# A hybrid decoder step on one core: routing rebuilt, new tokens second in w_o, last logits from unnormed rows

## The reference

```python
    return m @ w_o, conv_new, s_new.astype(h.dtype), vn
...
    x = x + g1 * mix
    h = rmsnorm(x, norm2) * (1 + sc2) + sh2
    x = x + g2 * hier_moe(h, w_rg, b_rg, w_re, b_re, w_e_gate, w_e_up, w_e_down)
```

## Time and profile before

| | us |
|---|---|
| median of 3 runs | 1181.98 |
| lowest, highest | 1181.97, 1183.64 |
| the profiled execution | 1181.74 |
| its span, first to last instruction | 1180.0 |

### The profile page before, as it was taken

One profiled execution on the slowest core, in us unless ns is written; L12 is line 12 of the kernel. 1 busy time (PEld: TensorE's weight loads), 2 busy tenths in 40 slices (PEclk: granted clock), 3 DMA queues, 4 the chain that ended last, 5 costly groups with the idle time before them and its releaser, 6 DMA issues. The chain is left out here.

```text
span 1180.0 us, 15016 instructions
## 1 busy us (share of the span) xinstructions
PE 1069.7 (91%) x5862; PEld 703.7 (60%) x5862; DVE 560.2 (47%) x1109; ACT 250.2 (21%) x673; POOL 154.4 (13%) x299
## 2 busy tenths in 40 slices
PE   5999998999999999899999999999946998978786
PEld 3455777777777887887577777754423333322222
DVE  3123737467788494475754455443264111110126
ACT  3100010567622222464111010101110110100011
POOL 3000500012314000041100000100011211111101
PEclk8999998999999999899999999999967999998998
DMA  9995543252414443124462422359176999999975
GB/s 334 340 258 181 192 77 75 43 128 69 74 50 72 107 80 73 37 73 144 125 223 83 111 75 89 123 138 327 77 286 222 416 420 415 418 419 418 412 290 175
DMA packets 96852, 226.32 MB, mean 192 GB/s; under 512 B 21422, under 2 KB 40167, under 8 KB 84082
## 3 DMA queue, kind: packets, MB, share of 16 engines
q1 hardware_dynamic: 86998, 202.70, 52.5%
q10 hardware_dynamic: 4660, 12.75, 3.1%
q0 software_dynamic: 5120, 9.88, 2.3%
HBM read 210.60 MB, written 23.08 MB: 198 GB/s over the span
## 5 line engine op out<-in xcount | busy, mean ns | idle before, releaser
L2514 PE MATMUL ps<-w_gate_up,xT 128*64 128x512 f32 x528 | 129.5, 630 | 20.5 <-DMA w_gate_up<-w_e_up 20.5
L2514 PEld LDWEIGHTS ps<-w_gate_up,xT 128*64 128x64 f32 x528 | 41.2, 145 | 105.9 <-issue 76.8
L2676 DVE TENSOR_TENSOR act<-silu_gate,ps 128x256 f32<-128x256 f32 x17 | 7.1, 420 | 199.1 <-ACT silu_gate L2469 199.1
L695 PE MATMUL ps<-hT,w_ring 128*128 128x288 f32 x384 | 97.5, 414 | 3.7 <-PEq L105 3.7
L695 PEld LDWEIGHTS ps<-hT,w_ring 128*128 128x128 f32 x384 | 73.9, 195 | 23.9 <-issue 4.0
L2531 PE MATMUL ps<-w_down,actT 128*64 128x512 f32 x264 | 62.1, 599 | 8.8 <-DVE actT L2680 8.8
L1345 PE MATMUL ps<-hT,w_ring 128*128 128x288 f32 x264 | 67.8, 407 | 0.0
L1630 DVE SCALAR_TENSOR_TENSOR conv_y<-z_staged,convT,conv_y 128x600 f32<-128x600 f32 x72 | 59.7, 842 | 9.3 <-ACT conv_y L1080 7.5
L1345 PEld LDWEIGHTS ps<-hT,w_ring 128*128 128x128 f32 x264 | 49.4, 190 | 13.1 <-issue 0.5
L2531 PEld LDWEIGHTS ps<-w_down,actT 128*64 128x64 f32 x264 | 18.0, 136 | 41.2 <-issue 29.1
L2429 POOL DMA_INDIRECT pair_scratch<-y_block,pairs x16 | 16.0, 1003 | 200.7 <-ACT y_block L2477 200.7
(11 more groups left out here) (539 smaller groups left out, 1995.2 us busy)
## 6 DMA issues: line engine op xcount, KB each, us to landing
w_down<-w_e_down SPq DMA_DIRECT2D x32, 1024.0 KB, 23.6
w_ring<-w_in SPq DMA_DIRECT2D x15, 2048.0 KB, 13.8
w_gate_up<-w_e_gate SPq DMA_DIRECT2D x30, 1024.0 KB
w_gate_up<-w_e_up SPq DMA_DIRECT2D x30, 1024.0 KB
w_ada_slots<-w_ada SPq DMA_DIRECT2D x8, 2048.0 KB, 8.4
w_ada_slots<-w_ada SPq DMA_DIRECT2D x4, 1024.0 KB, 15.0
w_ring<-w_pa SPq DMA_DIRECT2D x2, 2048.0 KB, 7.9
w_ring<-w_pb SPq DMA_DIRECT2D x2, 2048.0 KB, 7.9
```

The source lines that it names most:

```text
L695: last = nc.tensor.matmul(psum[:, bank + hf, 0:HALF], w[:, c, 128 * q:128 * q + 128], x[:, c, HALF * hf:HALF * hf + HALF], start=c == 0, s ...
L2514: last = te.matmul(psum[side(u), s % 2, :], xT[:, s % 2, c, side(u)], gu[s % GU_BUFS][:, u, :, c, :], start=c == 0, stop=c == KC - 1)
```

## The change

In this order of the program:

- Positions: `ORDER = (0, 4, 1, 2, 3)`. Everything between w_o and the weights is kept by position, with the new tokens at position 1 and tile 3 last. `mod_new` is needed at position 1.
- TensorE's order in w_o: the transposes of position p-1 stand between the two halves of position p, its logits between the first and the last four chunks of the second half.
- Position 1 carries a 65th row, the prompt's shift, whose logits (with the bias) are spread to all rows by one matmul (`constant_logits`).
- The last tile's `h` is first written as x times scale, half by half (`scaled`), transposed and multiplied by the router from that; the row factor and the constant logits are applied on the 36 logits (L2551). The square is taken by halves, and GpSimd adds two instructions to join them.
- Routing by parts: `choose_experts` for three positions between the last tiles' residual adds, with its counts in memory of their own; `split_pairs` and `slot_rows_of` for these stand between the two halves of the last residual add. The same for the last two positions afterwards. Slots come from counts to which 1024 is added at every odd expert, so that one comparison finds side and slot, and the table of 16 columns holds the experts' first 64 rows only.
- Further blocks have a table of their own: `over_blocks` ahead of `weights`, `over_counts` and `over_pairs` behind the first `xT`, `over_slots` in block 1 ahead of its activation, 20 matmuls (`over_tables`) behind block 1's gate and up, two conversions behind them. GpSimd waits for it before the gather of block 8.
- SP: the first expert of `w_down` 3 is loaded without a wait; the second waits for `route_constants_used`, which VectorE gives at the end of `over_slots`. Block 3's `w_gate_up` stands behind it.
- GpSimd: `x_gathered` isn't cleared any more, `y_last` is cleared behind the first two gathers.

```diff
+ORDER = (0, 4, 1, 2, 3)
+EARLY_POS = 3
+SIDE = 1024.0
...
+        sp.wait_ge(xwd, 2)
+        sp.wait_ge(xsq, NT + 1)
         sp.wait_ge(x2st, 16 * NT)
         load_down(sp, m, ins, 2, (4, 5))
-        sp.wait_ge(h2tr, NT)
+        sp.wait_ge(h2d, NT)
+        sp.wait_ge(h2tr, END)
+        sp.wait_ge(x4tr, 2)
...
+        whole = range(KC)
+        o_half(0, 0, whole)
+        o_half(0, 1, whole)
+        o_new(1)
+        h2_transposes(0)
+        o_half(2, 0, range(0, 2))
+        logits(0)
+        o_half(2, 0, range(2, KC))
+        for p in range(2, NT):
+            if p > 2:
+                o_half(p, 0, whole)
+            h2_transposes(p - 1)
+            if p == 3:
+                constant_logits()
+            o_half(p, 1, range(0, 4))
+            logits(p - 1)
+            o_half(p, 1, range(4, KC))
+        early_counts()
+        last_transposes(0)
+        logits(END, range(0, 4))
+        table(0, EARLY_POS)
+        last_transposes(1)
+        logits(END, range(4, KC))
+        late_counts()
+        table(EARLY_POS, NT)
...
+        residual(0, 0)
+        residual(0, 1)
+        second_norm(0)
+        dve.wait_ge(nld, 32 * NB)
+        v.scalar_tensor_tensor(modn[0:64, 2, :], modn[0:64, 2, :], 1.0, n2[0:64, :], ALU.add, ALU.mult).then_inc(sc2, 1)
...
+        residual(3, 1)
+        dve.wait_ge(ld, 3)
+        choose_experts(nc, dve, m, r, 0, EARLY_POS, 0)
+        second_norm(3)
+        choose_experts(nc, dve, m, r, 0, EARLY_POS, 1)
+        residual(END, 0)
+        scaled(0)
+        split_pairs(nc, dve, m, r, 0, EARLY_POS)
+        add_logits(3)
+        slot_rows_of(nc, dve, m, r, 0, EARLY_POS, psum[:, 2, 0:96])
+        residual(END, 1)
+        scaled(1)
...
     def sync(sp):
-        sp.wait_ge(overd, 1)
-        load_down(sp, m, ins, 3, (6, 7))
+        load_down_of(sp, m, ins, 3, 0, 6)
+        sp.wait_ge(constd, 1)
+        load_down_of(sp, m, ins, 3, 1, 7)
...
+            last.then_inc(over_hot, 1)
+            dve.wait_ge(over_hot, 1)
+            v.nop().then_inc(constd, 1)
...
         def run(lo, hi):
+            if lo == 0:
+                over_blocks()
+                weights()
             x_evacuate(lo)
+            if lo == 0:
+                over_counts()
+                over_pairs()
             for s in range(lo, hi):
+                if s == 1:
+                    over_slots()
                 dve.wait_ge(sgd, s + 1)
+                if s == 1:
+                    over_table_columns()
```

More of the change, by code:

```diff
@@ new lines, in slot_rows_of, with step @@
+def slot_rows_of(nc, dve, m, r, lo, hi, counts):
+    v = nc.vector
+    at, n = slice(lo, hi), hi - lo
+    def step(i):
+        r.n += 1
+        i.then_inc(r.step, 1)
+        dve.wait_ge(r.step, r.n)
+    dve.wait_ge(r.counted, 1 if lo == 0 else 2)
+    for k in range(2):
+        i = v.tensor_tensor(r.prod[:, k, at, :], r.one[:, k, at, :], counts.rearrange("p (t e) -> p t e", e=NE), ALU.mult)
+        if k:
+            step(i)
+    for k in range(2):
+        i = v.tensor_reduce(r.v[:, k, at], r.prod[:, k, at, :], AX.X, ALU.add)
+        if k:
+            step(i)
+    for k in range(2):
+        for p in range(lo, hi):
+            last = v.tensor_scalar(r.onehot_slot[:, k, p, :], m.slots[:, :], r.v[:, k, p:p + 1], None, ALU.is_equal)
+    last.then_inc(r.hot, 1)
@@ L2096, in scalar, with square @@
-        square(0)
[L2097 to L2100, removed]
+        act.wait_ge(init, 3)
+        act.wait_ge(mld, 32)
+        act.wait_ge(win, 7 * PAIRS)
+        a.copy(h2[64:65, 1, :], modp[64:65, 1, :]).then_inc(shd, 1)
+        def square(p):
+            rows = PROWS[p]
+            act.wait_ge(x2d, 2 * p + 2)
+            if p:
+                act.wait_ge(xsq, p)
+            a.activation(junk[0:rows, :], m.x2[0:rows, ORDER[p], :], ACT.Square, accum_out=ss[0:rows, p:p + 1]).then_inc(xsq, 1)
@@ new lines, in keep_half @@
+        def keep_half(j):
+            act.wait_ge(x4tr, j + 1)
+            act.wait_ge(lmm, END)
+            a.copy(h2T[:, 4 * j:4 * j + 4, :].rearrange("p c t -> p (c t)"), psum[:, 4 + j, :]).then_inc(h2ev, 1)
+        square(0)
+        for p in range(1, END):
+            store_h2(p - 1)
+            keep_h2T(p - 1)
+            square(p)
+        store_h2(END - 1)
+        keep_h2T(END - 1)
+        square_half(0)
+        keep_half(0)
+        square_half(1)
+        keep_half(1)
+        store_h2(END)
@@ L2175, in tensor, with o_half @@
[L2175 to L2181, removed]
+        def o_half(p, j, cs):
+            tile, i = ORDER[p], 2 * p + j
+            if i >= 4 and cs[0] == 0:
+                pe.wait_ge(oev, i - 3)
+            for c in cs:
+                last = te.matmul(psum[:, i % 4, :], mT[:, c, tile_cols(tile)], wo[j][:, c, :], start=c == 0, stop=c == KC - 1)
+            if cs[-1] == KC - 1:
+                last.then_inc(omm, 1)
@@ new lines, in late_counts, with table @@
+        def late_counts():
+            pe.wait_ge(r.chosen, 2)
+            te.matmul(psum[:, 3, 0:32], r.strict, both[:, 3, :], start=False, stop=False)
+            te.matmul(cut(psum[:, 3, 32:96]), r.onesb, two(both[:, 3, :]), start=False, stop=False)
+            te.matmul(psum[:, 3, 32:64], r.strict, both[:, 4, :], start=False, stop=False)
+            te.matmul(psum[:, 3, 64:96], r.onesb, both[:, 4, :], start=False, stop=True).then_inc(r.counted, 1)
+        def table(lo, hi):
+            pe.wait_ge(r.hot, 1 if lo == 0 else 2)
+            for p in range(lo, hi):
+                rows = PROWS[p]
+                for k in range(2):
+                    for x in range(2):
+                        last = te.matmul(psum[:, 2, 128:144], r.onehot_slot[0:rows, k, p, :], r.parts[0:rows, x, k, p, :],
+                                         start=p == k == x == 0, stop=p == END and k == x == 1)
+            if hi == NT:
+                last.then_inc(r.tabled, 1)
@@ L2260, in vector @@
         dve.wait_ge(init, 2)
[L2262 to L2290, removed]
```

535 lines of the change are left out of this document (333 added, 202 removed).

## The result

| | before | after |
|---|---|---|
| median of all runs, us | 1181.82 (20 runs) | 1186.82 (20 runs) |
| lowest, highest | 1178.11, 1186.24 | 1182.84, 1190.53 |
| span of the profiled execution | 1180.0 | 1184.9 |

The ratio of after to before is 1.0043, with a 95% interval of 1.0032 to 1.0053: the changed kernel is slower by 5.0 us. The forecast was 1185.7, so the sign and the range hold, and the size was 1.3 us short if the two shifts are compared (+5.0 against +3.7).

What follows compares the result with a forecast made beforehand. The prediction took the restart of the expert weight stream and the bytes then left as the bound. Wait +2.5, 1 MB +2.5 and early traffic -1.3 gave 1181.98 + 3.7 = 1185.7 us, range 1179.0 to 1189.5.

Steps and rivals of the forecast that it cites:

- Link 1: TensorE's w_o stage, up to its last matmul: ends at 864.9 us instead of 861.4, +3.5 us.
- The stall on `mod_new`: In w_o, new tokens' modulation usable only at 810.5 us: VectorE stands 4.8 us, TensorE waits +3.4 us.
- Link 2: From the end of w_o to the routing table: 16.7 us instead of 29.8, `toks` ready at 881.6 us.
- Link 3: First gather, issued amid weight loads: 8.4 us to landing instead of 4.6, at 890.3 us instead of 896.05.
- The even share of bytes: First gather sharing engines evenly with the weights: 5.8 us, forecast 2.6 us lower; the prediction set it aside.
- Link 4: From the gather to the end of block 0's gate/up matmuls: unchanged 12.5 us, ending 902.8 us instead of 908.5.
- Link 5: SP waits for the signal after `over_slots`, at 911.1 us against a restart at 908.56; sum +3.7 us at the last weight.
- The 2.5 us for the 1 MB: Weight stream: 1 MB formerly loaded in idle time now goes in front of block 3, +2.5 us.
- The -1.3 us: Scatter 0 and gather 3 start some of their traffic before the weight stream restarts, -1.3 us.
- No stall: Rival in w_o: the modulation loads land before 806 us, -5.3 us, giving 1180.4 us; chance 15%.
- Light gather: Rival at the first gather: it takes only 4.6 to 7 us, giving 1181.9 to 1184.3 us; chance 15%.
- TensorE carries: Rival in the expert stage: the stream has slack and TensorE sets the end, giving 1178.3 us; chance 8%.

Runs made afterwards that it cites:

- the run with clear engines: Changed kernel, but SP waits for the first gather's landing before loading w_gate_up 2 and the first expert of w_down 3; 1182.39 us, ratio 0.9993.
- the early signal: Changed kernel with over_slots moved ahead of block 0's activation instead of in block 1; 1178.97 us, ratio 0.9975 to the kernel before.
- the second experiment: Changed kernel with SP's first expert weights held until the 16 loads of mod_new have landed; 1183.04 us, ratio 1.0004 to the kernel before.
- the late restart: Kernel before, with block 3's gate/up load also waiting for block 0's down matmuls; ratio 1.0047.

## Why the prediction was right, and where it was off

**Link 1, the end of w_o, +3.5: right, +3.6 by the traces** (865.02 - 783.94 = 81.1 us against 77.5). The stall on `mod_new` was foreseen in its place, and a little small: usable at 812.0 us instead of 810.5, so VectorE stood 6.2 instead of 4.8 us and TensorE 4.5 instead of 3.4. The last bytes moved later: the last packet of the sixteen loads ended at 811.4 us, where it had ended at 809.8 us in the kernel before (queue q10 had 1.04 MB by 809 us there, and 1.02 in the changed kernel), and VectorE started 0.6 us behind it, so the 1.5 us that were put behind 809 us fitted the kernel before. In three other executions of kernels with the same w_o it ended from 810.5 to 811.5 us. The slow clock came out as assumed, one stretch (four chunks in 5.40 us) in the place of the one before. That the total is right is in part luck: the 1.1 us more of waiting was made up by the set of transposes and logits that came into w_o, priced at 2.9 us. It is that of the new tokens, and took 0.92 + 0.92 us (820.82 to 821.74 and 826.98 to 827.90). The 0.5 us for constant logits and a wait for `h` was too much as well; the constant logits took 0.3 us and TensorE didn't wait there.

**Link 2, 16.7 us: right.** 865.02 to 881.68 us is 16.7. Small VectorE instructions at their interpolated pitch (64 elements 0.26 us, as 877.27, 877.53, 877.79 in the trace) carry such a sum well.

**Link 3, the gather, 8.4 us: mis-sized, 9.3 measured** (881.97 to 891.27 us). This is the first of the steps that made the forecast short. The mechanism was right and shown by the run with clear engines. The scatters of the earlier trace rows were the nearest rows but transfers in the other direction in a steadier stream; four kernels with weights in the queues now give 9.2 to 9.6 us from the request to TensorE's start. The even share of bytes that would have given 5.8 us was rightly set aside.

**Link 4, 12.5 us, "unchanged": 13.1.** It wasn't unchanged. TensorE had stood 10.0 us, the clock was at 0.50 up to 895 us, and the rows for the last block took 4.36 us. In the kernel before, behind a wait of 6.2 us, they took less, at a clock of 0.50 in the stretch from 895 to 900 us too:

```profile
897.86 3.64 PE L2540 MATMUL ps<-ident,slot_rows 128*128 128x128 f32 x20
```

The longer wait alone doesn't explain it. These twenty matmuls took 4.36, 4.14 and 4.23 us behind waits of 10.0 to 10.3 us, but with the early signal 3.44 us behind a wait of 9.9 us, and 3.37 to 3.69 us in the five kernels with waits of 5.0 to 6.4 us. What decides it stays open; the link was taken over from the kernel before without a range for its clock. The gate/up matmuls ended at 904.35 us, where 902.8 was forecast.

**Link 5, SP's new wait: right in mechanism, signal 1.5 us later for the reasons above.** From the end of gate/up to `over_slots` 3.1 us (3.0 forecast), `over_slots` 5.1 us (5.3), and 0.4 us more for issuing the 1 MB load ahead of block 3's, which the sum had left out. Restart 913.0 instead of 911.1 us. The 2.5 us for the 1 MB fits this kernel (208.1 - 205.6); the others with it gave 2.1 to 4.2. The -1.3 us, traffic of scatter 0 and gather 3 done before the restart, was too much. Scatter 0 was issued at 911.43 us, and nothing of it moved before 913.0 us; the first packet of the weights moved at 913.75. From 913 to 913.5 us GpSimd's queue moved

```profile
q0 software_dynamic: 46, 0.19, 95.3%
```

so some 0.7 us of the engines' time was used before the weights, not 1.3.

Sum by the traces: +4.4 (restart, from w_o's start) + 2.5 (1 MB) = +6.9, where +5.1 was measured; forecast +2.5 + 2.5 - 1.3 = +3.7. In the two profiles the difference lies behind the last request for weights: from there to the end the profile before took 65.9 us and the profile after 63.8. Over the nine profiles this stretch took 63.8 to 65.9 us without following the edits, and what sets it stays open. So the chain that the prediction follows was 3.2 us short (1.9 at the restart, 1.3 in the credit for early traffic), and 1.8 of them were given back by something that it doesn't hold.

**The rivals.** "No stall" was priced at -5.3 us; made true by the second experiment it gave -4.6, and -6.9 on top of the early signal. "Light gather" was priced at -3.8 us for a gather of 4.6 us; made true by clear engines (4.4 us) it gave -5.9 (3.7 to 8.1), and -4.4 on top of the early signal. "TensorE carries" is refuted by the late restart. The two prices were fair within the noise, for things that didn't happen by themselves. No run took the rebuilt routing itself back out; that it made the table 9.5 us earlier is read from the two traces.

## What to carry to other kernels

Where a prefetched stream stops for want of buffers, find what its restart waits for and read every wait that a change adds on the queue of that stream: a signal given 8 us later than needed cost more than the rebuilt routing had gained (9.6 us at the table, 4.9 behind the slower gather), and giving it from idle time of the same engine turned the change around. A small transfer on the critical path should be issued before, or into a gap between, the large ones; here both losses to load order (the modulation in w_o, the first gather) went away by holding back bulk loads that had slack. Price a shortened link together with its next link, since the gather now fell among weights that it had missed before.

## What the runs showed of the hardware

The modulation's 16 small loads slow down far more than their own bytes. In the changed kernel they run beside the weights, and with the modulation first they run alone. The stretches 786 to 799 and 800 to 810 us, first of the changed kernel:

```profile
786.00:799.00 13.00, 13.00 (x29) 5.62 (x28) 1.39 (x2) 1.04 (x1) 0.00 (x0) 0.93 1.06 212
800.00:810.00 10.00, 10.00 (x52) 4.50 (x49) 3.54 (x4) 2.16 (x3) 0.76 (x2) 1.00 1.04 213
```

then of the kernel with the modulation first:

```profile
786.00:799.00 13.00, 13.00 (x28) 5.62 (x27) 1.87 (x3) 1.04 (x1) 0.00 (x0) 0.89 0.47 63
800.00:810.00 10.00, 10.00 (x46) 3.86 (x45) 6.52 (x8) 1.96 (x3) 0.77 (x2) 1.00 0.93 356
```

With them in the queues the engines are full (share 1.06) but move 212 GB/s, half of the 418 of the expert stage; alone, the 1.05 MB take 14 us (784.1 to 798.3) at a share of 0.47, that is 7.5 of 16 engines at a time, and 63 GB/s; without them the weights come at 356 GB/s at once. The kernel before shows the same beside its weights (226 GB/s from 786 to 799 us). In the changed kernel the loss ends with them. The weights' queue, from 786 to 799 us and from 812 to 820 us:

```profile
q1 hardware_dynamic: 313, 2.24, 90.2%
...
q1 hardware_dynamic: 391, 2.92, 87.2%
```

A packet of the weights took 0.60 us (0.902 x 16 x 13 / 313) beside the small loads and 0.29 us behind them, though the small loads' own share was only about 15% (queue q10). The 0.45 MB that q10 moved from 812 to 820 us, 13.9% of the engines' time, did the weights no such harm, so it isn't the second queue as such. What it is stays open; no run changed the form of these loads.

A gather issued into full engines waited 4.4 us for its first packet, and 1.9 us with clear ones. A lone idle span of TensorE of 4.5 us was followed by 1.75 us of extra time in the next matmuls, and its removal brought both back.
